# Moving every buffer from h_hi on by 192 bytes within SBUF

## What is computed

```python
# first block
h = rms_norm(x, norm_mix);  proj = h @ w_in
y = concat([gdn_mixer(...), dsa_mixer(...), conv_mixer(...)])      # gated delta rule, top-k attention, convolution
x = x + y @ w_out
x = x + memory_cross_attention(rms_norm(x, norm_cross), rms_norm(mem, norm_mem), ...)
x = x + square(relu(rms_norm(x, norm_mlp) @ mlp_w1)) @ mlp_w2      # 1024 -> 4096 -> 1024
# second block
h = rmsnorm(x, ln1_g);  proj = h @ w_in_2                          # 1024 -> 7168, with convolutions and an RG-LRU
merged = sigmoid(gate_a) * (y_a @ w_out_a) + sigmoid(gate_b) * (y_b @ w_out_b)
x = x + merged @ w_o
h = rmsnorm(x, ln2_g)
x = x + (silu(h @ w_ffn_gate) * (h @ w_ffn_up)) @ w_ffn_down       # 1024 -> 2816 -> 1024
return rmsnorm(x, final_g)
```

## Time and profile before

| | us |
|---|---|
| median of three runs | 1804.88 (1802.97 to 1805.49) |
| the profiled execution, whole | 1805.38 |
| the profiled execution, span from the first to the last instruction | 1803.3 |
| TensorE busy in the span | 1699.9 (94%) |
| VectorE / ScalarE / GpSimd busy | 980.0 / 643.5 / 254.2 |
| mean granted TensorE clock | 0.958 of full |
| moved by DMA | 146.35 MB, 81 GB/s over the span |

### The profile page before, as it was taken

One profiled execution on the slowest core, in us unless ns is written; L12 is line 12 of the kernel. 1 busy time (PEld: TensorE's weight loads), 2 busy tenths in 40 slices (PEclk: granted clock), 3 DMA queues, 4 the chain that ended last, 5 costly groups with the idle time before them and its releaser, 6 DMA issues.

```text
span 1803.3 us, 22119 instructions
## 1 busy us (share of the span) xinstructions
PE 1699.9 (94%) x7754; PEld 1379.5 (76%) x7754; DVE 980.0 (54%) x1378; ACT 643.5 (36%) x923; POOL 254.2 (14%) x154
## 2 busy tenths in 40 slices
PE   6899999578998999999999999999999999999996
PEld 5688798456875888888887888888788888888885
DVE  4666599843645643244435766666545544444333
ACT  2341423223435432134324444445322433334221
POOL 7745559920000000000000000000000000000000
PEclk8899999667999999999999999999999999999998
DMA  5212100100120222322222333333222222222332
GB/s 206 96 59 71 47 31 6 70 12 1 60 80 24 90 96 95 97 88 93 101 90 65 95 97 93 95 85 101 98 93 93 93 93 93 93 93 79 105 96 70
DMA packets 44705, 146.35 MB, mean 81 GB/s; under 512 B 4720, under 2 KB 5872, under 8 KB 44656
## 3 DMA queue, kind: packets, MB, share of 16 engines
q1 hardware_dynamic: 42240, 140.62, 24.3%
q10 hardware_dynamic: 2416, 5.08, 0.8%
HBM read 143.32 MB, written 2.10 MB: 81 GB/s over the span
## 4 chain that ended last, share of the span: by engine, by line
PE 85%; DVE 11%; issue 2%; ACT 2%; DMA 1%; ACTq 0%; DVEq 0%; SPq 0%
PE acc L615 76%; DVE c_acc L1934 2%; PE acc L917 1%; DVE tok L1915 1%; DVE d_score_a L1920 1%; DVE g_x L1911 1%; PE acc L676 1%; DVE m_lo L1697 1%; DVE g_xt L1917 0%; PE acc L929 0%; DVE d_score_b L1920 0%; PE acc L808 0%; PE acc L1069 0%; ACT a_p L1522 0%; DVE qkv L1745 0%
## 5 line engine op out<-in xcount | busy, mean ns | idle before, releaser
L615 PE MATMUL acc<-h_hi,w_hi 128*128 128x512 f32 x1248 | 501.4, 402 | 5.2 <-DVE h_lo L1727 5.2
L615 PE MATMUL acc<-h_hi,w_lo 128*128 128x512 f32 x1248 | 495.0, 397 | 0.0
L615 PE MATMUL acc<-h_lo,w_hi 128*128 128x512 f32 x1248 | 494.9, 397 | 0.0
L1686 DVE TENSOR_TENSOR w_lo<-raw,w_hi 128x1024 fp32r<-128x1024 f32 (+1 forms) x244 | 286.4, 1176 | 81.6 <-ACT w_hi L1236 59.9
L1236 ACT ACTIVATE w_hi<-raw 128x1024 fp32r<-128x1024 f32 (+1 forms) x244 | 245.3, 1008 | 190.9 <-PE acc L615 108.6
L615 PEld LDWEIGHTS acc<-h_hi,w_hi 128*128 128x128 f32 x1248 | 237.0, 190 | 63.2 <-DVE h_lo L1727 7.2
L615 PEld LDWEIGHTS acc<-h_hi,w_lo 128*128 128x128 f32 x1248 | 236.7, 190 | 55.7
L615 PEld LDWEIGHTS acc<-h_lo,w_hi 128*128 128x128 f32 x1248 | 237.3, 190 | 54.6 <-issue 1.2
L615 PE MATMUL acc<-u_lo,w_hi 128*128 128x512 f32 x256 | 101.0, 395 | 0.0
L615 PE MATMUL acc<-u_hi,w_hi 128*128 128x512 f32 x256 | 101.0, 395 | 0.0
L615 PE MATMUL acc<-u_hi,w_lo 128*128 128x512 f32 x256 | 101.0, 395 | 0.0
(11 more groups left out here) (383 smaller groups left out, 2479.3 us busy)
## 6 DMA issues: line engine op xcount, KB each, us to landing
raw<-panels_a SPq DMA_DIRECT2D x112, 512.0 KB, 3.2
raw<-panels_b SPq DMA_DIRECT2D x68, 512.0 KB, 3.2
raw<-mix SPq DMA_DIRECT2D x48, 448.0 KB, 3.3
raw<-mix SPq DMA_DIRECT2D x16, 512.0 KB, 3.5
raw<-down SPq DMA_DIRECT2D x16, 384.0 KB, 3.1
raw<-down SPq DMA_DIRECT2D x16, 320.0 KB, 2.9
x<-xT ACTq DMA_DIRECT2D x4, 1024.0 KB, 8.6
outT<-x SPq DMA_DIRECT2D x8, 256.0 KB, 2.1
```

Source lines behind the costliest of these rows:

```text
L615: mm = e.matmul(out, w[:, w_at:w_at + wn], a, start=first and n == 0, stop=last and n == 2)
L1686: TTn(lo, raw, k.w_hi[:, ahead.slot(w)].bitcast(F32), ALU.subtract).then_inc(k.s_split_done, 1)
```

## The change

One line goes into plan_memory, between tok and h_hi. It raises top[0] to the next address that lies 192 bytes past a multiple of 512. top[0] was a multiple of 1024 there, so that h_hi and every buffer laid from h0 or r0 begins 192 bytes later. The buffers ahead of it (raw, w_lo, w_hi, x, const, vec, eps, rstd, sqacc, sq with ub over it, tok) stay where they are. No instruction changes but for the addresses in its operands.

```diff
@@ -205,6 +205,7 @@
     k.g_sq, _ = sb("g_sq", 2 * T, at=sq_end - 2 * T * 4)
     k.g_p, _ = sb("g_p", 2 * T, at=sq_end - 2 * T * 4)
     k.tok, _ = sb("tok", NTOK)
+    top[0] += (192 - top[0]) % 512
     h0 = top[0]
     k.h_hi, _ = sb("h_hi", KT * T, F32R)
     k.h_lo, _ = sb("h_lo", KT * T, F32R)
```

## The result

The changed kernel takes 1785.55 us (median of four, 1784.61 to 1787.76), the kernel before 1805.18 in the same comparison (four runs, 1802.97 to 1807.07); the ratio is 0.9882, 95% interval 0.9852 to 0.9912. The forecast was 1805.0, no change, with a range of 1803 to 1811. The gain of 19.6 us lies far outside it, on the side which the prediction held for the least likely.

The account below looks back on a forecast made before the run. TensorE's matmul count times start-to-start distance was taken as the bound. 1805.4 + 0 (TensorE) + 0 (other engines) + 0.1 (mem) = 1805.5; this execution lay 0.5 above the median, so 1805.0 us, range 1803.0 to 1811.0.

Parts of the forecast that it names:

- What bounds the kernel: Whole kernel: TensorE has 85% of the chain, so time is matmul count times start-to-start distance, 232.39 ns in L615.
- The term of TensorE: 6000 matmul starts of L615: no change in pace taken, bounds -0.7 to +2.7 ns each, -4 to +16 us.
- three places in the trace: L696 at 232.2 ns, six ub matmuls in 1.40 us, ya and yb at 233.3 ns: read as no address cost.
- The reason against 192: Streams of L615: 128 and 192 are multiples of 64, 416 is not, so L696 was nearest; 0 taken.
- Rival (c): L615 faster if 19 ns is an address clash: up to 114 us (1691), or 1 ns, 6 us (1799); chance 0.07.
- Rival (a): All 6000 starts slower, streams off multiples of 128 running as ub: 1.0 ns each, about +5.5 us, 1810.5; chance 0.20.
- The other terms: VectorE, ScalarE and GpSimd: cost 0, half a microsecond at most; transfers, first half of mem: +0.1 us.
- +0.1: First half of mem, a transfer at the start: cost taken in us, bounds 0 to +2.0.
- +0.75 estimate: First mem transfer by the Trainium skill's page: 38 beats instead of 32 for each 1024-byte piece, +0.75 us.
- The +2.0 us: First mem transfer slower, as if pieces needed three lines instead of two: up to 1807.0, counted in no change's 0.70.
- The yardstick: Whole kernel: 0.2%, 3.6 us, is what a measurement can tell from no change; 0.6 ns on each start.
- The 16.6 ns over the Trainium skill's figure: L615's pace against the page's 215.8 ns: left open; if a clash the change ends, 100 us less.

Follow-up runs that it names:

- the list: A kernel of its own, only L615-shaped matmuls: weights at 128 or 320, streams at 0 to 480 in steps of 32; 226.67 to 234.38 ns from start to start.
- the last list: A kernel of its own, only matmuls of 512 streamed columns: 128, 32 or 8 columns held, streams 0, 64, 128, 192 bytes past the weights; 226.7 to 233.3 ns.

## Why the prediction was wrong

**What bounds the kernel: right.** The long pieces of L615 carry the time; their counts stayed and their quotients moved, by 3.5 ns where the prediction would have been content with half of one. The test which the prediction named for itself (divide the long pieces by their counts) found the answer in two lines.

**The term of TensorE: the step that failed.** The prediction put TensorE's term at 0 ns for each of 6000 starts, with -0.7 as the least; it measured -3.48 ns. It took the 0 from three places in the trace. None of them was a sample of what it needed. L696 was read as "a stream at 128 runs as one at 0", so the stream's place doesn't matter. But it has the distance +128 and L615 has -128, and modulo 256 that is the same: L696 repeated the case and didn't vary it. ub at 416 has the distance 288, which is 32, one of the places with 233.3; its middle value of +1.0 ns was right (the list gives 233.33 for 32), and the prediction then explained it away with ya and yb. The bounds of -0.7 to +2.7 ns came from this one row and were put on all places; the measured term is -3.5 ns, or about -18 us behind 598 us.

**The reason against 192: an ordering with nothing behind it.** "Both are multiples of 64" made L696 the nearest row. The list shows that neither nearness nor roundness helps: 64 past the weights is good, 128 and 192 are not, and 4 bytes beside the best place lies the worst.

**Rival (c): the right quantity, at 0.07.** It named the 19 ns over 213.3, the distance of the two addresses, and the move from 128 to 64. It was put down because "distances of -128, +128 and 288 all show it", the same slip: three numbers that are two classes. Its span of 1 to 19 ns held the 3.5, though neither of the two times it gave (1799 and 1691) is near 1785.55. The experiments confirm its place, not its cause: a clash that grows with the columns loaded should have gone with 8 columns and didn't.

**Rival (a)** had the price right for its condition (ub's pace on all starts) and the condition wrong. It is what the kernel with 64 in place of 192 shows, 233.35 ns; L697 is a small case of it inside the changed kernel (m at 192, weights at 128: distance -64).

**The other terms.** VectorE and ScalarE kept 692 to 694 and 632 ns, as predicted. GpSimd's 31 taps have a median of 1108 ns, where it was 1042, with the minimum at 1035 ns for 1032. Most of them lie near 1040 or near 1367 ns in both kernels, and the median sits at the upper edge of the first group. The kernel with the weights at 0, in which c_y has its old place in its line, has 1112, so this is not the offset. For mem the runs can't settle the prediction's +0.1, nor its +0.75 estimate: the median landing took 4.7 us for 4.4, but with mem at its old place three other executions had 4.9, 4.3 and 5.8. The +2.0 us didn't come: in this execution mem isn't even on the chain, where const stands in its place:

```profile
2.21 7.98 DMA const<-const
```

**The yardstick.** The prediction held 0.2% (3.6 us) for a change that can be told. Nineteen executions of the kernel before in the later comparisons went from 1799.3 to 1812.0 us, 0.7%, with the longer ones at the lower granted clocks (0.954 to 0.959 for the nine above 1808, 0.958 to 0.966 for the ten below 1804). A gain of 6 us, its small form of rival (c), would have been hard to see in four runs; the quotients of the long pieces, which agree to 0.01 ns, are the better measure.

**The 16.6 ns over the Trainium skill's figure.** The Trainium skill's formula for 512 columns, 215.8 ns ("TensorE: Matmul & The Clock Gate", "Back-to-back issue gap"), was set against the trace, and the gap of 16.6 ns was left open. The same section of the Trainium skill calls this the gap of an isolated matmul and puts a sustained stream of loads and matmuls at about 131 ns; no place in these runs reaches either figure, the lowest being 226.67. The surplus was the room in which this change works: the best place gets 5.7 ns of it back.

## What to carry to other kernels

When a kernel is a long row of equal matmuls, take the time from start to start, compare it with columns over clock, and treat what is left over as something that addresses can move: here it spread from 226.7 to 237.2 ns, and a one-line shift of a buffer was worth 1.2% and the best one tried 1.8%. What counted was the place of the streamed operand against the held one modulo 256 bytes, so both must be laid out together; starting both at the same place modulo 256 was the best of all that were tried. And before rows of a trace are used to bound an effect, write down for each the quantity that could matter, here a difference modulo something, and see whether the samples differ in it at all.

## What the runs showed of the hardware that was not expected

- float32r matmuls of 512 columns, 128 columns held, full clock: 226.67 ns from start to start with both operands at the same place modulo 256, 228.89 at 64 past, 232.4 to 234.4 at the other multiples of 32, 237.2 at 4 past. Distances 0, 64, 128 and 192 gave the same paces in a list of nothing but matmuls and in whole kernels; 4 past was seen in the list alone.
- The pace is a repeating pattern rather than a fixed interval, and one address pair can have two of them: 232.4 and 233.3 at distance 128, 228.9 and 233.3 at distance 64. Which one runs may change within an execution and from one execution to the next: at distance 64, with ub at 224, the same 1560 matmuls took 364.00 us in one and 357.09 in another. At distance 0 no second one was seen in the profiled executions of three kernels.
- Fewer held columns don't take the surplus over 213.3 ns away: 32 columns gave 230.5 to 231.7 ns at all four distances, 8 columns 226.7 to 231.7.
- The record of a weight load lasts 192 ns for 128 columns, 108 for 32 and 88 for 8 (the last list): by an estimate from these three, 0.83 to 0.88 ns a column on some 81 ns that don't shrink.
- The granted clock in the front moves the whole kernel. Three executions at distance 64 had 122.9, 126.3 and 136.5 us at 1.2 GHz ahead of the first long piece, which began at 592.9, 597.4 and 598.9 us; two at distance 128 had 133.1 and 139.9 us, and it began at 598.9 and 604.6.
